# State updates and convolution rows ahead of the group norm, variance ahead of the centring, and two up-projection units taken in turns

## The reference, cut to what matters

```python
h = x @ p['w_in']                                  # 20 tiles of 128 rows
ya = rms_norm(s5_branch(...)); yb = rms_norm(stick_breaking(...))
yc, ret_s = retention_branch(...)                  # o = group norm of o; s = decay * s + k^T v
mix = jnp.concatenate([ya, yb, yc], axis=-1) @ p['w_out']
x = layer_norm(ALPHA * x + mix, p['ln1_g'], p['ln1_b'])
f, conv_new = conv_ffn(x, conv_prev, p['w_up'], p['conv_w'], p['conv_b'], p['w_down'])
x = layer_norm(ALPHA * x + f, p['ln2_g'], p['ln2_b'])

def conv_ffn(x, prev, w_up, conv_w, conv_b, w_down):
    h = x @ w_up                                   # 5632 columns: 44 tiles of 128
    hp = jnp.concatenate([prev, h], axis=1)
    c = conv_b + sum(conv_w[j] * hp[:, j:j + L] for j in range(CONV_W))   # CONV_W = 3
    a, gate = jnp.split(c, 2, axis=-1)
    return (jax.nn.silu(gate) * a) @ w_down, hp[:, -(CONV_W - 1):]
```

## Time and profile before

| what | value |
| --- | --- |
| time, median of 3 runs | 719.52 us (719.36 to 722.17) |
| the profiled execution's own time | 719.84 us |
| its span | 717.9 us |
| PE busy | 676.0 us, 94% of the span |
| DVE, ACT, POOL busy | 557.1, 412.6, 154.2 us |
| granted clock of TensorE, mean of the span | 0.992 of full |

### The profile page before, as it was taken

One profiled execution on the slowest core, in us unless ns is written; L12 is line 12 of the kernel. 1 busy time (PEld: TensorE's weight loads), 2 busy tenths in 40 slices (PEclk: granted clock), 3 DMA queues, 4 the chain that ended last, 5 costly groups with the idle time before them and its releaser, 6 DMA issues.

```text
span 717.9 us, 13323 instructions
## 1 busy us (share of the span) xinstructions
PE 676.0 (94%) x5054; PEld 621.0 (86%) x5054; DVE 557.1 (78%) x1107; ACT 412.6 (57%) x673; POOL 154.2 (21%) x116
## 2 busy tenths in 40 slices
PE   5998999998999999998999989999899999999994
PEld 4766877996999999997997777889799999999993
DVE  6979972899998888599968996059999888873543
ACT  4666433866766666643565704475676666653343
POOL 0000002331222222644220000212212222245441
PEclk9999999999999999999999999999999999999997
DMA  9556611364667555544457364236546555555411
GB/s 351 191 209 205 197 64 59 123 209 127 206 217 242 189 184 179 163 144 149 145 161 250 109 213 145 63 124 233 157 148 208 198 182 177 178 178 209 158 55 60
DMA packets 41522, 121.34 MB, mean 169 GB/s; under 512 B 5043, under 2 KB 14163, under 8 KB 40947
## 3 DMA queue, kind: packets, MB, share of 16 engines
q1 hardware_dynamic: 39746, 115.55, 47.8%
q0 software_dynamic: 704, 3.06, 1.8%
q10 hardware_dynamic: 1008, 1.89, 0.7%
HBM read 115.00 MB, written 5.48 MB: 168 GB/s over the span
## 4 chain that ended last, share of the span: by engine, by line
PE 69%; DVE 17%; ACT 2%; issue 1%; ACTq 0%; DVEq 0%
PE ps L390 17%; PE ps L391 17%; PE ps L392 16%; PE ps L383 9%; PE ps L429 2%; DVE w_lo L1363 2%; DVE x_lo L1316 1%; DVE z L1277 1%; DVE work L1517 1%; DVE work L1518 1%; PE ps L599 1%; PE ps L491 1%; PE ps L518 1%; PE ps L499 1%; PE ps L684 1%
## 5 line engine op out<-in xcount | busy, mean ns | idle before, releaser
L390 PE MATMUL ps<-x_hi,w_hi 128*128 128x264 f32 x672 | 191.6, 285 | 6.7 <-DVE x_lo L1316 5.2
L391 PE MATMUL ps<-x_lo,w_hi 128*128 128x264 f32 x672 | 190.4, 283 | 0.0
L392 PE MATMUL ps<-x_hi,w_lo 128*128 128x264 f32 x672 | 190.3, 283 | 0.0
L849 ACT CAST w_hi<-ring 128x1024 fp32r<-128x1024 f32 x144 | 149.5, 1041 | 62.1 <-PE ps L392 61.0
L1363 DVE TENSOR_TENSOR w_lo<-ring,w_hi 128x1024 fp32r<-128x1024 f32 x118 | 146.5, 1242 | 29.8 <-ACT w_hi L849 27.5
L390 PEld LDWEIGHTS ps<-x_hi,w_hi 128*128 128x128 f32 x672 | 126.5, 188 | 9.1 <-issue 4.9
L383 PE MATMUL ps<-x,ring 128*128 128x264 f32 x544 | 127.8, 390 | 0.8 <-ACT hb L1071 0.8
L391 PEld LDWEIGHTS ps<-x_lo,w_hi 128*128 128x128 f32 x672 | 126.6, 188 | 0.0
L392 PEld LDWEIGHTS ps<-x_hi,w_lo 128*128 128x128 f32 x672 | 126.0, 187 | 0.0
L383 PEld LDWEIGHTS ps<-x,ring 128*128 128x128 f32 x544 | 101.1, 190 | 23.0 <-issue 4.4
L390 PE MATMUL ps<-hff_hi,w_hi 128*128 128x264 f32 x352 | 101.6, 289 | 4.6 <-DVE w_lo L1363 4.6
(11 more groups left out here) (307 smaller groups left out, 1076.9 us busy)
## 6 DMA issues: line engine op xcount, KB each, us to landing
ring<-in_units SPq DMA_DIRECT2D x188, 512.0 KB, 3.6
kv<-in_kpool SPq DMA_DIRECT2D x32, 128.0 KB, 2.4
kv<-in_vpool SPq DMA_DIRECT2D x32, 128.0 KB, 2.6
SR<-in_sret SPq DMA_DIRECT2D x2, 1024.0 KB, 5.9
out_rsample<-SR POOLq DMA_DIRECT2D x2, 1024.0 KB, 4.7
z<-in_xT SPq DMA_DIRECT2D x2, 528.0 KB, 5.5
out_kv<-hb ACTq DMA_DIRECT2D x2, 528.0 KB, 4.4
out_y<-x SPq DMA_DIRECT2D x2, 528.0 KB, 2.7
```

The costliest lines, as they stand in the source:

```text
L390: mm(out, wh, hi, start=start, stop=False)
L391: mm(out, wh, lo, start=False, stop=False)
L392: return mm(out, wl, hi, start=False, stop=stop)
L849: E.did(nc.scalar.copy(w_hi[:, split_slot(i)], ring[:, ring_slot(n)]), "w_hi")
```

## The change

It has five parts.

- `ret_states` of samples 0 to 3 and the three convolution instructions (now a function `conv_prev`) stand on DVE ahead of `gn_center`, samples 4 to 7 right behind it. For that `v_samples` and `v_spread` come sooner: in the first layer behind input unit 16, into banks 6 and 7; in the second layer behind unit 16 too (before 17), still in banks 2 and 3.
- `ln_tail_up` makes the variance (`ln_rate`) ahead of any centring, centres five tiles while ACT works on the rate, and centres the other three behind the first three instructions on the tiles. `ln_nmr`, which only the corrections need, goes behind the tiles.
- Scale and bias of the tiles are on DVE for tiles 0 and 4 alone (X_DVE); ACT has six tiles in place of four.
- PE takes the first two split up units (UP + 2 and UP + 3) in turns, tile by tile of x, in place of one after the other.
- The `split_lo` of these two units stand one step sooner among the residuals, both ahead of residual 7.

```diff
+VB_BANK = [6, 2]
+X_DVE = [0, 4]
@@ PE @@
+                pair = (RAW_UP, RAW_UP + 1)
+                outs = [claim(i % 4, "up_free", L, i + 1)[:, 0:T] for i in pair]
+                for k in range(KT):
+                    need(pe, "x_lo", L, k + 1)
+                    for i, out in zip(pair, outs):
+                        if k == 0:
+                            wait_low(pe, L, UP + i)
+                        ins = split_product(out, UP + i, k, x_hi[:, k], x_lo[:, k], k == 0, k == KT - 1)
+                        if k == KT - 1:
+                            E.did(ins, "used")
+                for i in range(RAW_UP + 2, N_UP):
...
@@ ACT, ln_up @@
-                for t in range(1, KT, 2):
-                    needq(act, "xn", q, t + 1)
-                    E.did(f(x[:, t], z[:, t], ACT.Identity, scale=gb[:, t:t + 1], bias=gb[:, KT + t:KT + t + 1]), "xo")
-                    upper(t - 1)
-                    upper(t)
+                for p in range(0, KT, 2):
+                    for t in (p, p + 1):
+                        if t in x_act:
+                            needq(act, "xn", q, t + 1)
+                            E.did(f(x[:, t], z[:, t], ACT.Identity, scale=gb[:, t:t + 1],
+                                    bias=gb[:, KT + t:KT + t + 1]), "xo")
+                    upper(p)
+                    upper(p + 1)
@@ DVE, ln_tail_up @@
-                needq(dve, "lnmu2", q, 1)
+                ln_rate(q)
                 ln_center(q, 0, 5)
-                ln_rate(q)
-                ln_center(q, 5, KT)
-                ln_nmr(q)
+                needq(dve, "lnr", q, 1)
+                E.settle()
...
                     ln_xn(t + 1)
-                    needq(dve, "xn", q, t + 1)
-                    E.did(ts(x[:, t], z[:, t], g[:, t:t + 1], b[:, t:t + 1], ALU.mult, ALU.add), "xe")
-                    if t > 0:
+                    if t in X_DVE:
+                        needq(dve, "xn", q, t + 1)
+                        E.did(ts(x[:, t], z[:, t], g[:, t:t + 1], b[:, t:t + 1], ALU.mult, ALU.add), "xe")
+                    if t == 0:
+                        ln_center(q, 5, KT)
+                        rest = E.last
+                    else:
                         low(t - 2)
                         low(t - 1)
+                ln_nmr(q)
                 raw_columns(q, 0)
                 raw_sum(q, 0)
@@ DVE @@
                 sb_sample_out(L)
+                ret_states(L, range(NS // 2))
+                conv_prev(L)
                 gn_center(L)
-                ret_states(L, range(NS // 2))
+                ret_states(L, range(NS // 2, NS))
                 s5_cat(L)
...
-                ret_states(L, range(NS // 2, NS))
                 split_lo(L, N_IN + 4)
...
-                    if i == 6:
-                        split_lo(L, UP + RAW_UP)
-                split_lo(L, UP + RAW_UP + 1)
+                    if i in (5, 6):
+                        split_lo(L, UP + RAW_UP + i - 5)
                 ln_tail_up(L)
```

More of the change, by code:

```diff
@@ L241, in in_bank @@
             return i if i < RAW else (i + 1) % 2
[L243 removed]
+        PERL = {"in_evac": N_IN - RAW, "x": KT, "turns1": HJ, "lnacc1": 2,
                 "lnacc2": 2,  "z": 16, "bb": 1, "tph": 2, "tab": 4, "cneg": 1, "bu": 4, "buev": 4,
@@ L255, in hybrid_step @@
                 "hff_hi": FT, "hff_lo": FT, "spre": 1,
-                "xe": KT // 2, "x_hi": KT, "x_lo": KT,
+                "xe": len(X_DVE), "xo": KT - len(X_DVE), "x_hi": KT, "x_lo": KT,
                 "w_hi": SPLITS, "used": UNITS}
@@ L513, in v_samples @@
                 for half in range(2):
-                    bank = claim(2 + half, "vbev", L, half + 1)
+                    bank = claim(VB_BANK[L] + half, "vbev", L, half + 1)
                     for b in range(4):
@@ L734, in _ @@
                         transposes(L)
+                    if L == 0 and i == at_["vb"]:
+                        v_samples(L)
                     if i == at_["inner"]:
@@ L752, in _ @@
                         ret_out(L)
-                    if i == at_["vb"]:
+                    if L > 0 and i == at_["vb"]:
                         v_samples(L)
@@ L937, in ln_up @@
                 act.wait_ge(S("st_sr"), 16 * (L + 1))
+                x_act = [t for t in range(KT) if t not in X_DVE]
                 def upper(t):
-                    if t % 2 == 0:
-                        need(act, "xe", L, t // 2 + 1)
+                    if t in X_DVE:
+                        need(act, "xe", L, X_DVE.index(t) + 1)
                     else:
-                        act.wait_ge(S("xo"), L * KT // 2 + t // 2 + 1)
+                        need(act, "xo", L, x_act.index(t) + 1)
                     E.did(nc.scalar.copy(x_hi[:, t], x[:, t]), "x_hi")
-                for t in range(1, KT, 2):
-                    needq(act, "xn", q, t + 1)
-                    E.did(f(x[:, t], z[:, t], ACT.Identity, scale=gb[:, t:t + 1], bias=gb[:, KT + t:KT + t + 1]), "xo")
-                    upper(t - 1)
-                    upper(t)
+                for p in range(0, KT, 2):
[6 more added lines that the diff above has]
+                    upper(p + 1)
                 for i in range(RAW_UP):
@@ L1035, in v_spread @@
                     need(act, "vb", L, half + 1)
-                    E.did(nc.scalar.copy(VBC[:, 4 * half:4 * half + 4], ps[:, 2 + half].rearrange("p (b e) -> p b e", b=4)),
+                    E.did(nc.scalar.copy(VBC[:, 4 * half:4 * half + 4], ps[:, VB_BANK[L] + half].rearrange("p (b e) -> p b e", b=4)),
                           "vbev")
@@ L1124, in _ @@
                         v_tokens(L)
+                    if L == 0 and i == at_["vb"]:
+                        v_spread(L)
                     if i == at_["sv"]:
@@ L1594, in ret_states, with conv_prev @@
                                   ALU.mult, ALU.add), "sr" if last else None)
+            def conv_prev(L):
+                dve.wait_ge(S("ld_prev"), 16 * (L + 1))
+                if L > 0:
+                    dve.wait_ge(S("st_conv"), 16 * L)
+                w0 = bcast(pv(L, "cw0", 0, N_UP), [P, N_UP, NS], 2)
+                w1 = bcast(pv(L, "cw1", 0, N_UP), [P, N_UP, NS], 2)
+                c10 = cout[:, :, 2:10]
+                E.did(tt(spre[:], prev[:, :, 0], w0, ALU.mult))
+                E.did(tt(c10, prev[:, :, 1], w1, ALU.mult))
+                E.settle()
+                E.did(tt(spre[:], spre[:], c10, ALU.add), "spre")
             def diagonals(buf):
@@ L1743, in _ @@
                 split_lo(L, N_IN + 3)
-                ret_states(L, range(NS // 2, NS))
                 split_lo(L, N_IN + 4)
[L1746 to L1754, removed]
-                E.did(tt(spre[:], spre[:], c10, ALU.add), "spre")
                 for i in range(N_OUT):
```

10 lines of the change are left out of this document (5 added, 5 removed).

## The result

The changed kernel takes 725.53 us (median; 722.71 to 727.74), the kernel before 721.15 beside it: a ratio of 1.0073, interval 1.0053 to 1.0092. In a second session the ratio was 1.0070 (1.0054 to 1.0086). It is about 5 us slower; 718.9 was predicted, with 721.4 as the upper end. The executions of the kernel before lie mostly near 719.5 or near 721.5, so that their median moves between the two from session to session; the ratio is the steadier measure.

What follows compares the result with a forecast made beforehand. PE was taken to bound the kernel, with DVE setting the pace around the layer norm. From 719.84 us, -1.6 (chain), -0.5 (output projection) and +1.5 (one clock fall) give 719.2, predicted as a 718.9 median; range 715.8 to 721.4.

Steps and rivals of the forecast that it cites:

- The steps around the output projection: States, convolution rows and v_samples moved around the output projection: gain of 0.5 us, 0.1 in the first layer, 0.4 in the second.
- The table load and the square: ACT, first layer: both come 0.58 us later, so PE's second rms starts at about 127.95 instead of 127.43.
- the state instructions delay the first layer by their full excess: Rival at gn_center: eight state instructions cost 1.1 us, sum 719.5; shares a chance of 0.13 with the down-projection rival.
- both fall: Rival at UP + 4: clock falls in both layers, 1.5 us each, 720.4 us, slower than before; chance 0.17.
- The chain of the layer norm: DVE from variance to UP + 4: first product 1.47 us sooner, UP + 4 gains 0.8 us a layer, 1.6 in both.
- the two gains together: Layer norm's chain, 1.6 us, plus output projection, 0.5 us: 2.1 us gained before any clock fall.
- Residual 7 and the shift: Output projection's end: 0.58 us wait before the shift goes in both layers; residual 7 comes 0.3 us sooner in the second.
- The turns: UP + 2 and UP + 3 on PE: small waits gathered into one of 2.8 us before UP + 4, gaining nothing themselves.
- My chance of one half a layer: Clock behind the new UP + 4 wait: chance one half per layer of a 1.5 us fall, one fall counted.
- The "next 122 us" without a wait: PE behind UP + 4: no waits for 122 us, so a clock fall goes fully into the time.
- The fall in the down-projection: Half clock behind the 2.36 us wait in the down-projection: near 1.6 us lost by such a fall, taken as 1.5.
- The rival that it might go away and bring 1.5 us: Down-projection: a 2 us shift removes its fall (-1.5) or adds one at the 2.11 us wait (+1.5); shares 0.13.

Runs made afterwards that it cites:

- Experiments 2: Changed kernel, with POOL's w_lo of the first two output units waiting until DVE is through with the convolution rows: 724.23 us, ratio 1.0045 to the kernel before.
- 3: Changed kernel, with POOL's subtraction for the first two output units replaced by weights times zero, one input instead of two: 721.22 us, ratio 1.0012 to the kernel before.
- 1: Changed kernel, with the samples' states and convolution rows back behind gn_center on DVE, v_samples still early: 721.47 us, ratio 1.0025 to the kernel before.
- 4: Kernel before with only v_samples, states, convolution rows and one split moved; layer norm and PE's order unchanged: 724.11 us, ratio 1.0045.
- 7: Changed kernel, with states, v_samples and their banks as before, conv_prev ahead of gn_scale, turns kept: 720.53 us, ratio 1.0003 to the kernel before.
- 8: Changed kernel, with states, v_samples and their banks as before, conv_prev ahead of gn_scale, without the turns: 717.88 us, ratio 0.9979 to the kernel before.
- experiment 11: The changed kernel again, unaltered, for a second profile: 725.12 us, ratio 1.0070 to the kernel before; the profiled execution took 727.41 us.
- 5: Changed kernel without the turns, PE taking UP + 2 and UP + 3 one after the other: 724.01 us, ratio 1.005 to the kernel before.

## Why the prediction was wrong, step by step

**The step that failed** is in "The steps around the output projection": DVE's wait for gn_means "fills them with 2.18 + 1.43 = 3.6 us, so gn_center comes 1.1 us later". 2.18 was read from the earlier trace rows, where the state instructions stand behind gn_center and POOL's subtraction (124.28 to 126.64) is over. This is POOL's row of the kernel before:

```profile
124.28 2.36 POOL L1827 TENSOR_TENSOR w_lo<-ring,w_hi 128x1024 fp32r<-128x1024 f32 x1 [0.90 <-ACT w_hi L849]
```

In front of gn_center the state instructions stand beside the subtractions. The term was 6.40 + 1.53: gn_center came 5.4 us later and the output units 4.2, not 0.5. Experiments 2 and 3 show that POOL's subtraction is the cause, 1 and 4 that it makes up most of the loss (with the falls that come with it), and 7 against the change that the states and v_samples back in place are worth 5 us.

The Trainium skill has the rule: SBUF — State Buffer, section Who interferes with whom, says that a VectorE instruction with two inputs in SBUF contends with a GpSimd instruction that reads SBUF. It calls the shared ports an exclusive lock, and says of VectorE's two-port modes that whoever issues first has them for its whole instruction. I had not weighed it. With two inputs on POOL this trace agrees: held instructions of 2.47 and 2.43 us, ending with POOL's. With one input the run departs from a lock for the whole instruction: 1.16 us at most, against POOL's 2.77, and nothing in the second layer.

In the kernel before, gn_center, with one input from PSUM, ran under the second subtraction and was not held: its four instructions took 0.43 us each, as without POOL (the 1.76 of the group stand in the second layer too, where POOL is done). That is why the old order was cheap. The trace of before also has an instruction that was held: DVE's w_lo at 151.51 takes 1.79 us where most take 1.22; it starts 0.04 behind an addition of POOL with inputs in SBUF (151.47). Laying POOL's rows beside DVE's would have shown both.

**v_samples and the rivals.** The table load and the square came late as forecast (the wait of 0.69 at 128.12). Of my rivals, "the state instructions delay the first layer by their full excess" had the right place with the wrong excess, 1.1 where it was 5.4; "both fall" had the right sign.

**The chain of the layer norm** was right. The first product with the rate stands 1.98 us behind the variance (167.41 to 169.39; 2.0 forecast, 3.48 before), and UP + 4 starts 14.31 behind it, 14.2 forecast. Without the turns it measures as a ratio of 0.9979, 1.6 us, against the 2.1 of the two gains together; but in that profile UP + 4 of the second layer is 3.1 us sooner than before, and 0.9 of it goes in the late landing of the output.

**Residual 7 and the shift** were right in kind: the 0.58 went in both layers, and residual 7 came 0.7 sooner where I had counted 0.3.

**The turns** made the wait of 2.83 us that was forecast as 2.8, and the fall behind it. A count over all profiles: of fourteen waits of 2.4 to 2.8 us in front of UP + 4 ten were followed by half the clock, and none of the ten of at most 0.65. My chance of one half a layer was low, and 1.5 us for both layers should have been about 2 (ten in fourteen, twice, 1.5 each); experiments 7 and 8 give 1.7 to 2.6. The "next 122 us" without a wait are 143, to 322.37; the argument stands.

**The fall in the down-projection** was priced at 1.5 us from the earlier trace rows. Where it stood it cost nothing, as the pairs of rows in experiment 11 show. The rival that it might go away and bring 1.5 us was therefore void. In five of the thirteen profiles the fall came one unit later instead, and there it costs 0.7 to 0.9. The fall that this rival feared behind the wait of 2.11 stands in two profiles (experiments 4 and 5), in neither of the changed kernel.

**The sum, as the two profiles have it** (start of the same row of PE, changed less before, in us):

| stretch | forecast | profile |
| --- | --- | --- |
| to the first output unit | +0.5 | +4.17 |
| from there to UP + 4, both layers | -2.6 | -2.72 |
| from UP + 4 to the second layer's output units, with one fall | +1.5 | +0.51 |
| behind the second UP + 4 | 0 | +1.04 |
| the span | -0.6 | +3.0 |

The first row is the collision. The second (1.6 for the chain, 0.58 for the shift, 0.4 for residual 7) is right. In the third, the fall's 1.3 us are in part taken up by two waits of before (0.53 at 322.37, and 0.88 at 389.44, now 0.40). The fourth, the late landing, I had put at nothing.

The changed kernel's other executions take 2 to 5 us more than the profiled one. In the second profile 4.2 of the 4.7 us more are falls of the clock, half of them behind the collision's own wait for RI: three of the four profiles with that wait of 2.5 us show a fall there, and the output units then start 1.0 us later for one fall (8.30 behind the product that waited, against 7.31) and 2.2 for two. What the middle executions have wasn't seen. That the collision brings these falls was seen in the profiles; it wasn't tried by itself, and why a wait of one length is followed by a fall in one execution and not in the next stays open.

## What to carry to other kernels

Before moving a VectorE instruction that reads two tiles from SBUF, lay GpSimd's time line beside its new place: a duration read from the trace holds only for the same neighbours. Gathering short waits of TensorE into one long one in front of a dense stretch is worth nothing by itself and may cost a stretch at half the clock; first take away what the long wait is for (here the order of one split, 3 to 4 us with the turns). And price a fall of the clock only where the next thing that TensorE waits for moves with it.

## What the runs showed of the hardware that was not expected

- One VectorE instruction of 0.34 us is held for 2.47 us by a GpSimd subtraction with two inputs from SBUF; the following ones run at full speed in the gap. The excess over the eight is 4.2 us for two subtractions of 2.35 and 2.48 us.
- With one input on GpSimd the excess is 0.8 us for an instruction of 2.77 us that starts 0.01 us ahead of them, and none for one that starts 1.0 us ahead.
- The number of stretches at 1.2 GHz changes from one execution of one kernel to the next: two in one profile of the changed kernel (722.71 us), five in the other, two of them without a gap between (727.41 us), not counting the one behind the last matmul that every profile has. One such stretch has 15 to 18 matmuls in 3.4 us where 28 to 30 fit.
- A fall at about 70 us, in seven of the thirteen profiles, leaves no delay that shows where it is a single one: PE's wait of 0.69 ends at 127.83 to 128.13 in three profiles with it, at 128.11 to 128.36 in four without.
- The last transfer of the output lands 2.7 us behind its issue in three kernels and 3.3 to 3.7 in ten, though its instruction, its shape and its distance from the last matmul are the same. The cause is open.
